# Head norms split between VectorE and GpSimd in a two-layer hybrid attention block

## The reference, cut to what matters

```python
def rms_norm(x, gain):
    x32 = x.astype(jnp.float32)
    y = x32 * lax.rsqrt(jnp.mean(x32 * x32, axis=-1, keepdims=True) + RMS_EPS)
    return (y * gain.astype(jnp.float32)).astype(x.dtype)
...
    q_a = partial_rotary(rms_norm(q_a, moba_q_gain), positions)
    k_a = partial_rotary(rms_norm(k_a, moba_k_gain), positions)
...
    o_c = from_heads(forgetting_attention(rms_norm(q_c, fox_q_gain), rms_norm(k_c, fox_k_gain),
                                          v_c, log_f))
...
    q = rms_norm(to_heads(q_flat, MEM_HEADS, MEM_HEAD_DIM), q_gain)
```

## Time and profile before

| | us |
|---|---|
| median of 3 runs | 1453.81 |
| lowest and highest run | 1452.18 and 1454.29 |
| the profiled execution's own time | 1453.06 |
| its span in the trace | 1451.3 |
| TensorE busy | 1378.5 |
| VectorE busy | 967.3 |
| ScalarE busy | 810.4 |
| GpSimd busy | 14.3 |

### The profile page before, as it was taken

How to read it: one execution, slowest core, us unless ns; L and a number is a source line. 1 busy time by engine, 2 the same in 40 slices (tenths; PEclk the granted TensorE clock), 3 DMA queues, 4 the chain that set the end, 5 groups by cost and what they waited for, 6 DMA issues and landing times.

```text
span 1451.3 us, 20526 instructions
## 1 busy us (share of the span) xinstructions
PE 1378.5 (95%) x6968; PEld 1157.8 (80%) x6968; DVE 967.3 (67%) x1499; ACT 810.4 (56%) x1312; POOL 14.3 (1%) x12
## 2 busy tenths in 40 slices
PE   4999999989999988999989999999899998899998
PEld 3888888868787867888878888888687876788887
DVE  4777656667877557776557776657678775577764
ACT  5767535535546437775456764455364553577653
POOL 0000000000100000000000000000010000000000
PEclk9999999999999999999999999999999999899999
DMA  7555654535454535556545555455264455265552
GB/s 266 174 173 181 213 187 163 198 110 191 143 172 148 174 116 165 182 173 211 196 134 186 173 197 202 159 176 202 89 216 147 148 173 174 71 216 176 187 194 83
DMA packets 157804, 248.20 MB, mean 171 GB/s; under 512 B 6288, under 2 KB 97696, under 8 KB 157728
## 3 DMA queue, kind: packets, MB, share of 16 engines
q1 hardware_dynamic: 156112, 242.83, 50.4%
q0 software_dynamic: 896, 3.16, 0.7%
q10 hardware_dynamic: 720, 1.25, 0.2%
HBM read 246.16 MB, written 1.06 MB: 170 GB/s over the span
## 4 chain that ended last, share of the span: by engine, by line
PE 89%; DVE 6%; issue 3%; ACT 2%; DMA 1%; DVEq 0%; SPq 0%; ACTq 0%
PE psum L459 30%; PE psum L501 23%; PE psum L519 19%; PE psum L502 11%; DVE ring_lo L1081 1%; PE psum L590 1%; PE psum L608 1%; ACT ring_hi L792 1%; PE psum L639 1%; PE psum L578 1%; DMA x<-in_x 1%; PE psum L479 1%; DVE gate L1351 1%; PE psum L595 0%; ACT gate L801 0%
## 5 line engine op out<-in xcount | busy, mean ns | idle before, releaser
L1081 DVE TENSOR_TENSOR ring_lo<-raw,ring_hi 128x1024 fp32r<-128x1024 f32 x464 | 555.2, 1208 | 279.8 <-ACT ring_hi L792 278.1
L792 ACT ACTIVATE ring_hi<-raw 128x1024 fp32r<-128x1024 f32 x464 | 481.0, 1044 | 366.5 <-PE psum L459 239.7
L501 PE MATMUL psum<-hT,ring_hi 128*128 128x512 f32 x1408 | 495.7, 397 | 2.2 <-DVE hT L1122 2.2
L502 PE MATMUL psum<-hT,ring_lo 128*128 128x256 f32 x1408 | 394.9, 280 | 0.0
L459 PE MATMUL psum<-ring_hi,hT 128*128 128x512 f32 x1024 | 325.3, 393 | 0.0
L501 PEld LDWEIGHTS psum<-hT,ring_hi 128*128 128x128 f32 x1408 | 265.5, 189 | 66.1 <-DVE hT L1122 3.0
L502 PEld LDWEIGHTS psum<-hT,ring_lo 128*128 128x128 f32 x1408 | 266.9, 190 | 0.1
L459 PEld LDWEIGHTS psum<-ring_hi,hT 128*128 128x128 f32 x1024 | 192.4, 188 | 41.5 <-issue 1.0
L459 PE MATMUL psum<-ring_lo,hT 128*128 128x512 f32 x512 | 199.4, 390 | 0.0
L834 ACT ACTIVATE small<-psum 128x256 f32<-128x256 f32 x176 | 67.3, 383 | 150.0 <-PE psum L502 149.8
L459 PEld LDWEIGHTS psum<-ring_lo,hT 128*128 128x128 f32 x512 | 96.2, 188 | 19.2
(11 more groups left out here) (168 smaller groups left out, 1183.9 us busy)
## 6 DMA issues: line engine op xcount, KB each, us to landing
raw<-in_w_ffn_in SPq DMA_DIRECT2D x88, 1024.0 KB, 5.2
raw<-in_w_in SPq DMA_DIRECT2D x64, 1024.0 KB, 5.1
raw<-in_w_ffn_out SPq DMA_DIRECT2D x44, 1024.0 KB, 4.8
raw<-in_w_branch SPq DMA_DIRECT2D x16, 1024.0 KB, 4.9
raw<-in_w_mem_kv SPq DMA_DIRECT2D x8, 1024.0 KB, 5.3
raw<-in_w_out SPq DMA_DIRECT2D x8, 1024.0 KB, 4.8
forget<-negc_rows POOLq DMA_DIRECT2D x2, 1024.0 KB, 10.6
memx<-in_mem SPq DMA_DIRECT2D x2, 512.0 KB, 4.9
```

The costliest lines, as they stand in the source:

```text
L501: pe.matmul(out[:, :], w[0][:, kc, :], hT_both[:, kc, :, :], start=kc == 0, stop=False)
L502: mm = pe.matmul(out[:, 0:SEQ], w[1][:, kc, :], hT[0][:, kc, :], start=False, stop=kc == KC - 1)
L792: act.activation(unit_out(0, step, k), view, ACT.Copy).then_inc(hi_done.sem, 1)
L1081: dve.tensor_tensor(unit_out(1, step, k), view, unit_out(0, step, k).bitcast(F32), ALU.subtract)\
```

## The change

The norm of five of the six blocks (qm, qa, ka, qc, kc; mk stays as it was) is cut in three. In `serve` VectorE does the reduce alone, into `head_sum`. GpSimd computes the factors from it into `head_rs` (two buffers in turn), with fifteen instructions on tiles of 128x16 or 128x8: mean plus epsilon, minus half of that, the seed, and three Newton steps of four instructions; all but the second are linked by semaphores. VectorE's scaling, and for qa and ka gain and rotation, become a task `normed` that waits for the factors, planned at the END of the following step (a first half of the next block: gate for qm, ka for qa, gate for ka, qc and kc). It stands in the list ahead of the other END tasks of that step. The END tasks of the norm's own step now follow the reduce directly. The lo that stood between gain and rotation goes back to its usual place. On GpSimd the factors of qm, qa and ka come before the forget gate's transfers in program order, those of qc and kc behind the mask's addition.

```diff
@@ -145,6 +145,8 @@
 
 _plan("norm", None, _step_of("mv"))
 _plan("pool", None, _step_of("va"))
+for kind, following in (("qm", ("gate", (1, 0))), ("qa", ("ka",)), ("ka", ("gate", (1, 1))), ("qc", ("gate", (3, 0))), ("kc", ("gate", (3, 1)))):
+    _plan("normed", kind, _step_of(*following))
 _plan("qkT", 0, _step_of("gate", (1, 0), 1))
 _plan("qkT", 1, _step_of("qc"))
 _plan("qkT", 2, _step_of("y", (3, 1)))
@@ -218,6 +220,11 @@
         ra = sb("ra", [P, 16])
         rb = sb("rb", [P, 16])
         hss = sb("hss", [P, 16])
+        head_sum = sb("head_sum", [P, 16])
+        head_ms = sb("head_ms", [P, 16])
+        head_rs = sb("head_rs", [P, 2, 16])
+        head_a = sb("head_a", [P, 16])
+        head_b = sb("head_b", [P, 16])
         mx = sb("mx", [P, 8])
         nmx = sb("nmx", [P, 8])
         den = sb("den", [P, 2, 8])
@@ -307,6 +314,9 @@
         taken_act = tally("taken_act", sum(k in BY_ACT for k in BLOCK_KIND.values()))
         taken_dve = tally("taken_dve", sum(k not in BY_ACT for k in BLOCK_KIND.values()))
         norm_mk = tally("norm_mk", 1)
+        head_sums = tally("head_sums", len(NORMED) - 1)
+        head_factors = tally("head_factors", len(NORMED) - 1)
+        pool_link = tally("pool_link", 13 * (len(NORMED) - 1))
         rotated = tally("rotated", 2)
         squares = tally("squares", 2 * len(NORMED))
         qkT_ps = tally("qkT_ps", 3)
@@ -330,7 +340,7 @@
         split_ps = tally("split_ps", 2 * len(TURNED))
         split_hi = tally("split_hi", 2 * len(SPLITS))
         split_lo = tally("split_lo", 2 * len(SPLITS))
-        VLINKS = 155
+        VLINKS = 95
         vlink = tally("vlink", VLINKS)
 
 
@@ -1042,8 +1052,38 @@
 
         @block.gpsimd
         def _(pool):
+            links = [0]
+
+            def link(L, ins):
+                links[0] += 1
+                ins.then_inc(pool_link.sem, 1)
+                pool.wait_ge(pool_link.sem, links[0])
+
+            def factors(L, kind):
+
+                i = NORMED.index(kind) - 1
+                dst, heads = HEAD_DST[kind]
+                n = NT * heads
+                r = head_rs[:, (L * (len(NORMED) - 1) + i) % 2, 0:n]
+                if i >= 2 or L > 0:
+                    pool.wait_ge(taken_dve.sem, taken_dve.at(L if i >= 2 else L - 1, release(NORMED[1 + i - 2 if i >= 2 else 4 + i])))
+                pool.wait_ge(head_sums.sem, head_sums.at(L, i + 1))
+                link(L, pool.tensor_scalar(head_ms[:, 0:n], head_sum[:, 0:n], heads / BW, EPS, ALU.mult, ALU.add))
+                pool.tensor_scalar(head_b[:, 0:n], head_ms[:, 0:n], -0.5, None, ALU.mult)
+                link(L, pool.tensor_scalar(r.bitcast(I32), head_ms[:, 0:n].bitcast(I32), -0.5, 1597463007.0, ALU.mult, ALU.add))
+                for step in range(3):
+                    link(L, pool.tensor_tensor(head_a[:, 0:n], r, r, ALU.mult))
+                    link(L, pool.tensor_tensor(head_a[:, 0:n], head_a[:, 0:n], head_b[:, 0:n], ALU.mult))
+                    link(L, pool.tensor_scalar(head_a[:, 0:n], head_a[:, 0:n], 1.5, None, ALU.add))
+                    last = pool.tensor_tensor(r, r, head_a[:, 0:n], ALU.mult)
+                    if step < 2:
+                        link(L, last)
+                last.then_inc(head_factors.sem, 1)
+
             pool.wait_ge(setup_loads, 16 * N_SETUP)
             for L in range(DEPTH):
+                for kind in ("qm", "qa", "ka"):
+                    factors(L, kind)
 
                 pool.wait_ge(negc_ready.sem, negc_ready.at(L, 1))
                 pool.dma_start(negc_rows, negc).then_inc(negc_stored.sem, 16)
@@ -1054,6 +1094,8 @@
                 own_tile = forget[:, :, :].rearrange("p h (three k) -> p h three k", three=3)[:, :, 0:3:2, :]
                 pool.tensor_tensor(own_tile, own_tile, mask[:, None, None, P:SEQ].to_broadcast([P, NH, 2, P]), ALU.add)\
                     .then_inc(forget_ready.sem, 1)
+                for kind in ("qc", "kc"):
+                    factors(L, kind)
 
 
 
@@ -1248,6 +1290,8 @@
             def task(L, stage, arg):
                 if stage == "norm":
                     norm_lo(L, 1, 4)
+                elif stage == "normed":
+                    normed(L, arg)
                 elif stage == "qkT":
                     dve.wait_ge(qkT_ps.sem, qkT_ps.at(L, arg + 1))
                     if arg == FOX:
@@ -1309,7 +1353,7 @@
                 elif stage == "zT":
                     split(L, f"z{arg}")
 
-            def head_factors(L, squared, heads):
+            def key_factors(L, squared, heads):
 
                 link(L, dve.tensor_reduce(hss[:, 0:NT * heads].rearrange("p (t h) -> p t h", t=NT),
                                           squared[:, :, :].rearrange("p t (h d) -> p t h d", h=heads), axis=AX.X, op=ALU.add))
@@ -1317,7 +1361,7 @@
                 link(L, dve.tensor_scalar(ms[:, 0:n], hss[:, 0:n], heads / BW, EPS, ALU.mult, ALU.add))
                 newton(L, rs[:, 0:n], ms[:, 0:n], n)
 
-            def serve(L, s, kind, arg, half, before_rotary=None):
+            def serve(L, s, kind, arg, half):
                 if kind == "f":
                     dve.wait_ge(used.sem, used.at(L, 2 * s + 2))
                     dve.tensor_scalar(fz, banks_of(s)[0][0:NH, 0:SEQ], own[0:NH, 0, FORGET_AT:FORGET_AT + 1], None, ALU.add).then_inc(taken_dve.sem, 1)
@@ -1356,40 +1400,45 @@
                     last.then_inc(taken_dve.sem, 1)
                 elif kind == "mk":
                     dve.wait_ge(squares.sem, squares.at(L, 2))
-                    head_factors(L, gate[:, 0], MH)
+                    key_factors(L, gate[:, 0], MH)
                     for t in range(NT):
                         rows = kmem[:, t, :].rearrange("p (h d) -> p h d", h=MH)
                         last = dve.tensor_tensor(rows, rows, rs[:, t * MH:(t + 1) * MH, None].to_broadcast([P, MH, MHD]), ALU.mult)
                     last.then_inc(norm_mk.sem, 1)
                 elif half == 1 and kind in NORMED:
                     dst, heads = HEAD_DST[kind]
-                    d = BW // heads
-                    banks = banks_of(s)
                     dve.wait_ge(squares.sem, squares.at(L, 2 * NORMED.index(kind) + 2))
-                    head_factors(L, dst, heads)
+                    dve.tensor_reduce(head_sum[:, 0:NT * heads].rearrange("p (t h) -> p t h", t=NT),
+                                      dst[:, :, :].rearrange("p t (h d) -> p t h d", h=heads), axis=AX.X, op=ALU.add)\
+                        .then_inc(head_sums.sem, 1)
+
+            def normed(L, kind):
+                dst, heads = HEAD_DST[kind]
+                d = BW // heads
+                banks = banks_of(_step_of(kind))
+                r = head_rs[:, (L * (len(NORMED) - 1) + NORMED.index(kind) - 1) % 2, :]
+                dve.wait_ge(head_factors.sem, head_factors.at(L, NORMED.index(kind)))
+                for t in range(NT):
+                    last = dve.tensor_tensor(dst[:, t, :].rearrange("p (h d) -> p h d", h=heads),
+                                             banks[t][:, :].rearrange("p (h d) -> p h d", h=heads),
+                                             r[:, t * heads:(t + 1) * heads, None].to_broadcast([P, heads, d]), ALU.mult)
+                last.then_inc(taken_dve.sem, 1)
+                if kind in ("qa", "ka"):
+                    dve.wait_ge(taken_dve.sem, taken_dve.at(L, release(kind)))
+                    at = MOBA_AT + (0 if kind == "qa" else HD)
                     for t in range(NT):
-                        last = dve.tensor_tensor(dst[:, t, :].rearrange("p (h d) -> p h d", h=heads),
-                                                 banks[t][:, :].rearrange("p (h d) -> p h d", h=heads),
-                                                 rs[:, t * heads:(t + 1) * heads, None].to_broadcast([P, heads, d]), ALU.mult)
-                    last.then_inc(taken_dve.sem, 1)
-                    if kind in ("qa", "ka"):
-                        dve.wait_ge(taken_dve.sem, taken_dve.at(L, release(kind)))
-                        at = MOBA_AT + (0 if kind == "qa" else HD)
-                        for t in range(NT):
-                            rows = dst[:, t, :].rearrange("p (h d) -> p h d", h=heads)
-                            last = dve.tensor_tensor(rows, rows, own[:, :, at:at + HD].to_broadcast([P, heads, HD]), ALU.mult)
-                        link(L, last)
-                        if before_rotary is not None:
-                            before_rotary()
-                        dve.wait_ge(trig_done.sem, trig_done.at(L, 2))
-
-                        halves = [dst[:, :, :].rearrange("p t (h d) -> p t h d", h=heads)[:, :, :, 8 * i:8 * i + 8] for i in range(2)]
-                        tables = [v[:, :, None, :].to_broadcast([P, NT, heads, 8]) for v in (cosv, sinv)]
-                        for i, (a, b) in enumerate(((0, 0), (1, 1), (1, 0), (0, 1))):
-                            last = dve.tensor_tensor(rot[:, i], halves[a], tables[b], ALU.mult)
```

(20 more changed lines are left out.)

## The result

The changed kernel takes 1460.69 us, median of 5 runs (1459.5 to 1463.87), against 1453.81 us, median of 5, of the kernel before: ratio 1.0057, 95% interval 1.0039 to 1.0074. It is slower, on the side that was forecast, and 2.3 us from the forecast time of 1463.0. The loss is 6.9 us between the medians, against 9.9 forecast. The profiled execution took 1459.67 us, its span 1457.9 us, 6.6 more than before.

The account below looks back on a forecast made before the run. TensorE, busy 1378.5 of 1451.3 us, bounds the kernel. Terms -0.85 + 1.6 - 1.0 - 2.8 - 1.9 = -4.95 per layer, 9.9 slower for two, on 1453.06 give 1463.0 us; range 1438.5 to 1485, the forecast's own 1454 to 1470.

Parts of the forecast that it names:

- The bound and the order: TensorE bounds; 24 us off VectorE is worth nothing by itself, the new order counts; qa's stall moves to the scores.
- C: Price of GpSimd's fifteen-instruction chain: 0.30 us each, 4.5 us in all, bounds 3.15 and 6.3.
- The sharing: VectorE's instructions with both inputs in SBUF (los, 1.15 us apart, and shares) hold GpSimd out for their whole length.
- qm, qa, kc: Per-layer terms of three norms: qm loses 0.85 us, qa gains 1.6, kc loses 1.9.
- ka: Per-layer term: values product starts at 344.5 instead of 343.49, a loss of 1.0 us.
- qc: Per-layer term: y step waits 4.9 us for the scaling and the clock falls, a loss of 2.8 us.
- The sum: Five norms' terms together: 4.95 us lost per layer, 9.9 slower for two, 1463.0 us.
- Rival 1: No sharing between GpSimd and the los: gain of 7.0 us per layer, 1439.1 us; chance 0.27.
- Rival 2: Slow chain, over 5 us, with sharing: each further microsecond costs five per layer; at 5.5, 1480 us; chance 0.22.
- Rival 3: Fast chain of 3.15 to 3.6 us under sharing: 1450 to 1455 us; chance 0.13.
- rival 4: No gain in qa: another wait, ScalarE's pT, takes the place of L639's ahead of 317; chance 0.02.
- border of 2 us: A TensorE stand of 2 us or more makes its clock fall, costing about 1.8 us more.

Follow-up runs that it names:

- run 8: Kernel before, with VectorE's copy of pT in qa's second half-step moved between its two splits, ahead of the norm: 1441.53 us, ratio 0.9922 to the kernel before.
- run 5: Changed kernel with the scaling task placed behind the other END tasks of its step: 1447.79 us, ratio 0.9971 to the kernel before.
- run 3: Changed kernel with GpSimd's fifteen instructions replaced by fifteen memsets, root left out: 1438.63 us, ratio 0.9906 to the kernel before.
- run 1: Changed kernel with GpSimd's chain cut to one instruction, reciprocal root left out: 1438.13 us, ratio 0.9907 to the kernel before.
- run 2: Changed kernel with two Newton steps instead of three in GpSimd's chain: 1447.78 us, ratio 0.9974 to the kernel before.
- run 4: Changed kernel with VectorE computing the root right behind the reduce, scaling order kept: 1445.54 us, ratio 0.9955 to the kernel before.
- run 9: Kernel before, with GpSimd's mask addition to the forget tile cut in eight: 1450.96 us, ratio 0.9984 to the kernel before.

## Why the prediction held, and where its steps did not

**The bound and the order.** Right. The stall before was VectorE's queue, not its load (run 8 moves one copy and gets 11 to 12 us), and the change moved it instead of removing it: the split of the values stood behind `normed` (run 5).

**C.** Right. 0.30 us per instruction was taken; 0.22 + 0.08 and 0.26 + 0.08 were measured. Qa's fifteen took 6.5 us, 4.6 of it without what two meetings with splits added; no chain ran wholly undisturbed.

**The sharing.** Right in kind, shown by the changed kernel's trace and run 3. In size each meeting costs 0.8 to 1.1 us, as forecast for a split. One thing was missing: while VectorE runs share and splits back to back, GpSimd still gets one instruction in at each seam, four in qc, some 1.2 us that I had not counted.

**qm, qa, kc.** Right in layer 0 to 0.1 us. In layer 1 qa gained 0.5 instead of 1.6, since the clock stayed low for longer behind L605 (3.78 us, and the next half-step 0.9 us longer as well).

**ka.** The term was mis-sized. L649 waited 1.9 us, for which I had 1.4; and in layer 0 the clock fell behind it (2.85 us for L649, granted clock 0.66 in that stretch), which I had set to happen only from 2 us on:

```profile
343.50:346.40 2.90, 2.89 (x9) 2.42 (x10) 2.87 (x4) 0.00 (x0) 0.00 (x0) 0.66 0.79 249
380.00:382.00 2.00, 1.27 (x6) 1.07 (x7) 2.00 (x4) 0.41 (x1) 0.00 (x0) 1.00 0.95 330
1096.00:1098.00 2.00, 1.71 (x4) 1.43 (x5) 2.00 (x3) 0.00 (x0) 0.00 (x0) 0.50 0.36 139
```

(stretch, busy times as in the earlier trace rows, the granted clock is the last but two.)

**qc.** This step failed in layer 0. I had let GpSimd start when the exponentials end, because the reduce ended there in the earlier trace rows. That was the doing of the mask addition, which held VectorE's small instruction and so the reduce. In the changed kernel the addition came earlier against the scores, in layer 0 wholly, in layer 1 in part. VectorE's instruction and GpSimd's addition, layer 0, then layer 1:

```profile
367.78 0.17 DVE L1321 TENSOR_SCALAR nmx<-mx 128x8 f32<-128x8 f32 x1
...
361.95 4.57 POOL L1095 TENSOR_TENSOR forget<-forget,const 128x2048 f32<-128x2048 f32 x1 [7.89 <-DMA forget<-negc_rows]
...
1081.79 1.71 DVE L1321 TENSOR_SCALAR nmx<-mx 128x8 f32<-128x8 f32 x1
...
1078.84 4.63 POOL L1095 TENSOR_TENSOR forget<-forget,const 128x2048 f32<-128x2048 f32 x1 [9.31 <-DMA forget<-negc_rows]
```

Two things moved it in layer 0, by 4.0 us against the second transposes (from 7.9 us behind their start to 3.9). The stall in ka put TensorE 2.3 us later against GpSimd's transfers, which I had costed at nothing. And the load of the sums landed 1.7 us sooner: GpSimd waited 7.9 us for it and not 9.6. The wait was 9.3 us in layer 1 of the same trace and 9.1 to 10.0 in the traces of all other kernels; and in every one of those that has the addition in one piece VectorE's instruction is held, for 2.0 to 2.9 us. So the gain in layer 0's qc is partly paid for in ka and partly chance of the execution that was profiled; how often it comes was not measured.

In layer 0 GpSimd began the chain 2.7 us ahead of the share, the y step waited 1.6 us and ran at the full clock: a gain of 2.1, not a loss of 2.8. In layer 1 it had 1.2 us, the y step waited 3.1 and fell to half the clock (8.53 us): a loss of 2.4. That is near the forecast 2.8, but by other terms: a wait of 3.1 and not 4.9, and 3.1 us for the clock and not 1.8. I had the layers alike, since they were alike before.

**The sum.** 8.1 for both layers against 9.9 is nearer than its parts, and that is luck: over both layers ka's loss was forecast 2.6 us too small and qa's gain 1.0 too large, but qc's loss 5.3 too large. Another 1.5 us lies outside the norms. The direction does not rest on luck (runs 1, 2 and 4 show the chain as the loss); the closeness of the forecast time, 2.3 us, does.

**The rivals.** Rival 1 (no sharing) is out by the changed kernel's trace, where instructions of 0.22 us take 1.03 to 1.28 beside a split. Rival 2's slope, five microseconds per layer for one of chain, is what run 2 shows: 12 us for 1.2 over two layers. Rival 3 (a faster chain) is out by the measured pace, rival 4 by the 5.85 us wait that is gone from qa.

## What to carry to other kernels

On an in-order engine ask what stands behind a long piece of work before asking how to make it shorter: moving one copy ahead of the norm was worth 11 to 12 us, taking 22 us off VectorE cost 7. A chain of small dependent instructions handed to GpSimd took 0.3 us each here against VectorE's 0.21, plus about 1 us for every two-input VectorE instruction it meets; count those in the stretch where it will run, and plan it where nobody waits. And a row that is far over its like is worth following before it goes into a sum, since it may be of another size in the changed kernel, or from one execution to the next.

## What the runs showed of the hardware

- VectorE and GpSimd hold each other out for whole instructions in SBUF, both ways: a 128x16 multiplication on GpSimd goes from 0.22 to 1.28 us beside a split, two splits from 2.35 to 3.52 us beside GpSimd's pieces (run 9). Memsets on GpSimd are not held (0.11 us each, 0.17 apart).
- The length of a stand alone does not tell whether TensorE's clock falls behind it. In the changed kernel it fell after 1.93 us (ka, layer 0) and 3.1 us, and not after 1.87 us (ka, layer 1); in run 5 not after 2.26 us (L649, 1.97 us long, granted clock 1.00 from 336.9 to 339.0 us). In run 1 L605 waited 2.6 us in both layers, and the clock fell in layer 1 (2.86 us) and not in layer 0 (1.99). So the prediction's border of 2 us is not one. Where the clock fell, it cost 1.8 to 3.2 us.
- The second feed-forward took between 147.8 and 151.4 us in the traces of kernels that do not differ there, and differed by 2.3 us between two traces of one kernel.
